# Stick-breaking attention on TensorE: the tri sums from the end of one tick to the start of the next

## What is computed

```python
xn = RMSNorm(h); P = xn @ W_in
# group A: RWKV-7, 8 heads x 64, a delta-rule state that is scanned over time
S = (S * w_t[:, :, None, :] + sa[..., None] * (kk_t * a_t)[:, :, None, :]
     + v_t[..., None] * k_t[:, :, None, :])
# group B: stick-breaking attention, 8 heads x 64, in blocks of 128
z = jnp.einsum('bhqd,bhkd->bhqk', qb, kb) * scale
log_beta = jax.nn.log_sigmoid(z)
log_1m = jnp.where(mask, log_beta - z, 0.0)
log_a = log_beta + lax.cumsum(log_1m, axis=3, reverse=True) - log_1m
A = jnp.where(mask, jnp.exp(log_a), 0.0)
outs.append(jnp.einsum('bhqk,bhkd->bhqd', A, vb))
# then
h += RMSNorm(concat(A, B) @ W_out)
h += RMSNorm(relu(RMSNorm(h) @ W_up)^2 @ W_down)
```

## Time and profile before

| | |
|---|---|
| median of 3 runs | 1654.62 us (1652.13 to 1655.78) |
| the profiled execution: its own time | 1651.46 us |
| its span in the trace | 1649.8 us |
| mean granted clock of TensorE | 0.973 |
| busy: TensorE, weight loads, VectorE, ScalarE, GpSimd | 93%, 78%, 61%, 45%, 13% of the span |

### The profile page before, as it was taken

The page is one execution under the profiler, slowest core; times in us unless marked ns, Lnnn a source line. Parts: engine busy times, 40 slices in busy tenths (PEclk is TensorE's granted clock), DMA queues, the critical chain, the costliest instruction groups (busy, mean ns, idle before and its releaser), DMA issues. The chain is left out here.

```text
span 1649.8 us, 37238 instructions
## 1 busy us (share of the span) xinstructions
PE 1539.9 (93%) x15568; PEld 1287.1 (78%) x15568; DVE 1002.9 (61%) x1560; ACT 739.0 (45%) x1302; POOL 220.9 (13%) x256
## 2 busy tenths in 40 slices
PE   4999999995998989989869899999999999999997
PEld 3999999994777767767657777888888888888886
DVE  5123324424878877788674557555555666666666
ACT  6144435343777776777645444333334211111122
POOL 6423325320001011010122400000000000000000
PEclk7999999997999999999989999999999999999999
DMA  3333552646523315111044463233332432332235
GB/s 129 129 119 119 178 203 94 217 165 149 138 48 76 73 26 111 46 28 35 26 130 122 127 218 140 103 114 128 109 108 79 134 95 97 103 100 92 90 115 178
DMA packets 89964, 185.24 MB, mean 112 GB/s; under 512 B 7872, under 2 KB 48320, under 8 KB 89552
## 3 DMA queue, kind: packets, MB, share of 16 engines
q1 hardware_dynamic: 86064, 169.16, 33.1%
q10 hardware_dynamic: 3744, 13.85, 2.1%
HBM read 124.44 MB, written 57.49 MB: 110 GB/s over the span
## 5 line engine op out<-in xcount | busy, mean ns | idle before, releaser
L625 PE MATMUL inproj_acc<-xn_xh,inproj_wh 128*128 128x346 f32 (+1 forms) x624 | 207.8, 333 | 8.4 <-DVE inproj_wl L546 8.4
L625 PE MATMUL inproj_acc<-xn_xh,inproj_wl 128*128 128x346 f32 (+1 forms) x624 | 201.5, 323 | 0.0
L625 PE MATMUL inproj_acc<-xn_xl,inproj_wh 128*128 128x346 f32 (+1 forms) x624 | 201.3, 323 | 0.0
L546 DVE TENSOR_TENSOR inproj_wl<-xn_raw,inproj_wh 128x1024 fp32r<-128x1024 f32 x27 | 33.1, 1226 | 165.6 <-ACT inproj_wh L479 165.5
L625 PEld LDWEIGHTS inproj_acc<-xn_xh,inproj_wh 128*128 128x128 f32 x624 | 118.1, 189 | 12.1 <-ACT inproj_wh L479 8.8
L625 PEld LDWEIGHTS inproj_acc<-xn_xl,inproj_wh 128*128 128x128 f32 x624 | 118.1, 189 | 3.3 <-issue 1.9
L488 ACT ACTIVATE inproj_out<-inproj_acc 128x346 f32<-128x346 f32 (+1 forms) x78 | 35.8, 459 | 187.0 <-PE inproj_acc L625 187.0
L625 PEld LDWEIGHTS inproj_acc<-xn_xh,inproj_wl 128*128 128x128 f32 x624 | 118.2, 189 | 0.0
L2186 DVE TENSOR_TENSOR all_mh_f<-all_mh_f,tail_bank 128x512 f32<-128x512 f32 x112 | 76.9, 686 | 52.2 <-PE tail_bank L2338 50.4
L2186 DVE TENSOR_TENSOR all_ml_f<-all_ml_f,tail_bank 128x512 f32<-128x512 f32 x112 | 76.9, 686 | 51.9 <-PE tail_bank L2338 51.9
L2338 PE MATMUL tail_bank<-all_mh,tail_tl 128*128 128x512 f32 x256 | 100.9, 394 | 0.0
(11 more groups left out here) (288 smaller groups left out, 3973.8 us busy)
## 6 DMA issues: line engine op xcount, KB each, us to landing
tail_raw<-in_w_up SPq DMA_DIRECT2D x32, 512.0 KB, 4.4
u_scratch<-tail_c SPq DMA_DIRECT2D x64, 256.0 KB, 2.1
tail_raw_d<-in_w_down SPq DMA_DIRECT2D x32, 512.0 KB, 3.6
tail_raw_u<-u_scratch SPq DMA_DIRECT2D x32, 512.0 KB, 3.3
xn_raw<-in_w_in SPq DMA_DIRECT2D x28, 512.0 KB, 4.6
p_scratch<-inproj_out ACTq DMA_DIRECT2D x26, 520.0 KB, 2.7
chunk_scratch<-inproj_fields SPq DMA_DIRECT2D x4, 2720.0 KB, 9.2
mix_swp<-chunk_scratch SPq DMA_DIRECT2D x34, 256.0 KB, 5.1
```

What stands on the lines that cost most here:

```text
L546: w_low.done(dve.tensor_tensor(wl[s][:, :, :], raw[s][:, :, :], wh[s][:, :, :].bitcast(F32), ALU.subtract), "all")
L625: last = pe.matmul(acc[g][:, 0:size], w[s][:, kt, :], xx[:, kt, col:col + size], start=(kt == 0 and j == 0), stop=(kt == KD - 1 and j == 2))
```

## The change

In the list of quarters of `sticks` on TensorE, tri moves from the last quarter of a tick to the first quarter of the next: tri of task t ran at the end of tick t + 3 and runs at the start of tick t + 4, in front of that tick's z. The other engines' programs are untouched, and so are all waits and semaphores. In the changed file the lines behind it are 5 higher (z is L1345, turns L1353, pv L1372).

```diff
             def sticks():
                 for now in range(N + SB_LAG + 1):
+                    t = now - 4
+                    if is_task(t):
+                        soft_low.wait(pe, t)
+                        sums(tri, tri_r, t, at(t).first).then_inc(tri_done.sem, 1)
+                    yield
                     t = now
                     if at(t) is not None:
                         z_copied.wait(pe, t - 1)
...
                         last.then_inc(pv_done.sem, 1)
-                    yield
-                    t = now - 3
-                    if is_task(t):
-                        soft_low.wait(pe, t)
-                        sums(tri, tri_r, t, at(t).first).then_inc(tri_done.sem, 1)
                     yield
             program(lap, sticks)
```

## The result

The changed kernel takes 1644.54 us (median of 5 runs, 1640.36 to 1648.14) against 1654.62 before: ratio 0.9936, interval 0.9914 to 0.9958. Two repeats gave 0.9946 (0.9931 to 0.9961) and 0.9942 (0.9926 to 0.9958).

A forecast was written before the change was run, and what follows sets the result against it. The prediction took TensorE, busy for 93% of the span, as the bound. Its terms, -6.7 + 6.0 + 1.7 = +1.0 us, on the median of 1654.62 gave 1655.6 us, range 1648 to 1661.

The forecast's parts named there:

- At 556: Mix stage: the lap part starts 0.64 us earlier and tri follows without a wait; 0.64 of tri's 0.79 us kept.
- at 506: Mix stage: tri's 1.73 us wait becomes the lap part's and L1139 waits for tri; costs +1.7 us, or 0.5.
- at 439: Mix stage: rest no longer fills the lap part's wait for L957; 0.6 us lost per lap, +6.0 for ten.
- -6.7: Gain in us, mix stage: seventeen of twenty stick waits directly before lap parts keep something, 0.12 to 0.64 each.
- A: Rival: the losses vanish, as lap parts' products and next copies come earlier; -6.7 us remains, 1647.9 us; chance 0.26.
- B: Rival: lap parts arrive before their copies, over and over; +5.0 us, 1659.6 us; chance 0.22.
- C: Rival: TensorE's clock falls to 0.50 more often; sum +2.7 to +4.4 us, 1657.3 to 1659.0 us; chance 0.08.

The follow-up runs named there:

- e1: The changed kernel run again with no edit, for its time and a second trace; ratio 0.9946 to the kernel before.
- e4: The kernel before with only rest moved behind the lap part where it stood directly in front of one; ratio 1.0014.
- e9: The kernel before with the row tri, z, rest never cut by a lap part, its steps waiting until the lap part is done; ratio 0.9956.
- e3: The kernel before with only tri moved behind the lap part where it stood directly in front of one; ratio 0.9974.
- e11: The kernel before with the load of the output projection's weights queued three chunks later; ratio 0.9976, median 1649.21 us.

## Why the prediction was wrong

**What held.** The waits changed owners as forecast, by kind and nearly by size (1.9 for 4, 12.4 for 12 or more). At 556 and at 506 the lap part, tri and the wait stand as described; at 439 the lap part of e1 waits for L957, with rest behind it:

```profile
439.74 0.27 PE L1194 MATMUL mix_bank<-mix_xx,mix_nb 64*64 64x64 f32 x1 [0.32 <-ACT mix_xx L957]
```

The sum of the waits hardly moved: with the load moved, so without a standstill, TensorE's idle time is 37.6 and 37.3 us before and 36.4 and 35.2 in the changed kernel, 1.7 less on the mean, where the forecast's terms, all of them idle time, came to 1.0 more. tri and z are worth -4.3 and -5.8 alone, where -6.7 was put down for all waits together.

**The step that failed** is this one: "With nothing waiting it costs and gains nothing, since TensorE does both in either order." It prices order by idle time alone. In this stage the order changes how long the same matmuls take: by about 0.18 us for each lap part in the row tri, z, rest, by 0.27 for each wait in it beyond the wait itself (at 556, where the prediction kept 0.64 for the wait, this came on top), and over the stage, at full clock, by 14.3 us between e4 (388.2) and e9 (373.9). Tri's gain and rest's loss are of this kind, for e3 and e4 idle alike. In the changed kernel the busy time at full clock is 4.6 us less, 381.0 on the mean of its five traces (380.8 to 381.3) against 385.7 in the four of before (385.2 to 386.1), with the load at either place. As it was clocked it is 3.0 us less on the mean of the pairs with the load moved (392.2 against 395.2) and 3.3 on that of the others (392.6 in three traces against 395.9 in two), since the changed kernel ran longer at 0.50. With the load moved the 1.7 of idle time makes the stage 4.7 shorter; the medians differ by 2.3 and 4.6.

**The second omission** is the standstill. The earlier trace rows left out TensorE's waits without a releaser (5.3 us in 7 in that trace, the longest 2.1), and that one execution showed only 0.48 us of them at 431. In other executions before stands still there for 5.4 us, and moving one load is worth 4.2 and 6.9 us of its median (1653.45 to 1649.21, 1654.92 to 1648.01), to the changed kernel nothing. About half of the measured gain (2.3 and 4.6 us of 7.8 to 10.1 remain with the load moved, by the medians; 3.3 and 6.1 of 8.9 to 10.6 by the ratios) is therefore not the order's directly, but that the changed kernel does not pay for this load. The traces show how: before adds the standstill to its idle time (43.1 with it, 37.3 without), the changed kernel does not (37.3 and 36.4 with it, 37.5 without), so its other waits shrink by as much. At 439 the lap part that waits 0.32 us in e1 waits for nothing in the first trace, ten microseconds behind the standstill.

**The loss at 506** was put too high. The 0.5 of the step is there (the wait grew from 1.73 to 2.38), the further 1.2 is not: the L1139 that I read as waiting for this tri belongs to a task before. The earlier trace rows could have told: it starts at 506.56, while the tri begun at 506.10 runs until the lap part at 506.76. VectorE does wait for tri more, 12.3 us, but at other places and without TensorE's idle time growing.

**The rivals.** A's span (1644.0 to 1649.6) holds the time, by luck: the losses did not vanish, lap parts wait more than twice as long. B's waits came in part (12.4, not over 15), but the stick waits went by as much. C came in part: in four of the five traces of the changed kernel the clock falls to 0.50 behind the wait at 408, in none of the four of before. On the mean the stretches at 0.50 cost the changed kernel 11.4 us of busy time in the stage (10.1 to 13.0) and before 9.9 (8.7 to 11.7): 1.5 more, about what C put down for one stretch, though the ranges overlap, and less than the order gave. What C takes from the Trainium skill, page "TensorE: Matmul & The Clock Gate", stands there in the section "A second HAM failure mode: psum-queue depth-cycling".

**What stays open.** Where all of the 4.6 us of busy time went. The changed kernel has as many cuts as before (55, and with those between rest and tri 103 against 102); its nine row waits less, at 0.27 each, make 2.4, and the other 2.2 were not traced to rows. Why before's waits do not shrink behind a standstill as the changed kernel's do was not tried. That the load causes the standstill is shown by its going away with the load and by the late packets of q8, not by a run in which only those packets moved. And the load costs before more than its standstills: the lower half of its times beside e11 (1648.6 to 1653.5) also lies mostly above those with the load moved (1647.9 to 1652.2).

## What to carry to other kernels

Where two instruction streams are interleaved by hand on TensorE, look first at how long the same steps last in different neighbourhoods, from start to start: here a step of another tile shape in the middle of a row of like steps, or a wait there, cost time that no view of waits shows. Compare busy time over a stage between two traces before explaining a difference by waits, and take the clock out of it first: here that turned differences of 3.0 and 3.3 us into the same 4.6. And take waits without a releaser seriously: a second trace of the same kernel showed one of 5.4 us that the first had only as 0.48, and the queue of instructions in the DMA view showed what came late beside it.

## What the runs showed of the hardware

At full clock a 512-column step of two matmuls takes 0.47 us from start to start between steps of its own tile shape, 0.55 to 0.58 where a lap part of 64*64 matmuls, or pv, stands on one side of it, 0.66 with one on both sides, and 0.65 where the next like step waits. TensorE stood still for 1.7 to 5.4 us without a releaser at 428 to 436 us, in the middle of a lap part, in 10 of 13 traces with the load of the output projection's weights at its first place, and in none of five with it later. Each time it went on 1.4 to 1.7 us after a 16 KB packet of the instruction queue landed that had come 7.3 to 11.8 us after the one before.
